# Hybrid mLSTM, attention and expert step on one core: tile 0's experts fetched beside the later mLSTM cells, mixers in two sets of buffers

## What is computed

```
h  = modulate(rmsnorm(x))
z  = h @ w_in                      # mLSTM q, k, v, o, gates; attention q, k, v
mix = [ mLSTM forward + backward, normed, times sigmoid(o)  ||  attention with sink ]
x1 = x + gate1 * (mix @ w_out)
h2 = modulate(rmsnorm(x1))
q  = h2 @ w_q                      # 8 heads x 2 halves x 128
eidx, gates = top-16 of 16 x 16 sums of the top-16 of both halves' scores
a  = gelu(h2 . u[eidx]) ;  y = x1 + gate2 * sum(gates * a * v[eidx])
```

## Time and profile before

| | |
|---|---|
| runs | 3685.03, 3685.37, 3698.58 us; median 3685.37 |
| span of the profiled execution | 3682.8 us, first to last instruction (no separate time of this execution is recorded) |
| granted TensorE clock, mean | 0.865 of 2.4 GHz |
| moved by DMA | 1365.12 MB, mean 371 GB/s over the span |
| first expert fetch | 664.09 us |
| chain that ended last | DMA 40%, TensorE (PE) 20%, VectorE (DVE) 15%, issue 4%, POOL 4%, ScalarE (ACT) 4% |

### The profile page before, as it was taken

How to read it: one execution, slowest core, us unless ns; L and a number is a source line. 1 busy time by engine, 2 the same in 40 slices (tenths; PEclk the granted TensorE clock), 3 DMA queues, 4 the chain that set the end, 5 groups by cost and what they waited for, 6 DMA issues and landing times.

```text
span 3682.8 us, 31091 instructions
## 1 busy us (share of the span) xinstructions
PE 2644.4 (72%) x9770; PEld 1042.0 (28%) x9770; DVE 2453.7 (67%) x5523; ACT 990.0 (27%) x2700; POOL 1459.0 (40%) x1300
## 2 busy tenths in 40 slices
PE   7999888687877878866566567557656755775655
PEld 3455567333333333312121112112111211221111
DVE  3666435776787678648857677685767768576655
ACT  1223333442433244422122122212212221221111
POOL 0110023443454455434444444444444444444443
PEclk9999889899989989889799789879977987987677
DMA  7222446899999999999999999999999999999999
GB/s 299 95 97 94 163 125 204 333 410 422 416 421 426 425 412 420 389 424 414 427 427 427 427 423 427 422 417 424 416 427 420 427 420 423 424 417 427 411 427 380
DMA packets 224537, 1365.12 MB, mean 371 GB/s; under 512 B 25194, under 2 KB 36074, under 8 KB 75890
## 3 DMA queue, kind: packets, MB, share of 16 engines
q0 software_dynamic: 165888, 1208.03, 78.4%
q1 hardware_dynamic: 50992, 134.74, 10.1%
q10 hardware_dynamic: 7492, 20.36, 1.4%
HBM read 1334.05 MB, written 28.99 MB: 370 GB/s over the span
## 4 chain that ended last, share of the span: by engine, by line
DMA 40%; PE 20%; DVE 15%; issue 4%; POOL 4%; ACT 4%; SPq 0%; ACTq 0%; POOLq 0%; DVEq 0%
DMA fx_ring<-arg_uv,fx_eidx 38%; PE fx_acc L1396 11%; DVE fx_ring L1846 8%; POOL fx_ring L1109 4%; PE at_sP L1241 3%; ACT fx_weighted_pick L1542 2%; PE at_aP L1203 1%; DMA rt_wq<-arg_w_q 1%; DVE rt_rest L1708 1%; DVE rt_ab L1710 1%; DVE rt_rest L1706 1%; DMA rt_w_q<-arg_w_q 1%; PE at_sP L1269 1%; ACT fx_gelu L1538 1%; PE at_sP L1187 1%
## 5 line engine op out<-in xcount | busy, mean ns | idle before, releaser
L1396 PE MATMUL fx_acc<-fx_ring,fx_weighted_pick 128*64 128x512 f32 x4608 | 1417.7, 747 | 929.8 <-ACT fx_weighted_pick L1542 908.3
L1109 POOL DMA_INDIRECT fx_ring<-arg_uv,fx_eidx x1152 | 1317.0, 1143 | 1634.7 <-PE fx_acc L1396 1444.5
L1846 DVE CUSTOM_DVE_ANT_0 fx_ring<-fx_ring,fx_h 128x1024 f32<-128x1024 f32 x1152 | 1411.8, 1237 | 774.0 <-DMA fx_ring<-arg_uv,fx_eidx 769.5
L1396 PEld LDWEIGHTS fx_acc<-fx_ring,fx_weighted_pick 128*64 128x64 f32 x4608 | 327.0, 158 | 1903.7 <-ACT fx_weighted_pick L1542 1368.4
L1538 ACT ACTIVATE fx_gelu<-fx_dot 128x2 f32<-128x2 f32 x576 | 117.1, 203 | 2116.2 <-DVE fx_dot L1846 2115.7
L424 PE MATMUL in_z<-w_in,in_hT 128*128 128x512 f32 (+1 forms) x864 | 352.4, 566 | 7.3 <-PEq L97 7.3
L1542 ACT ACTIVATE fx_weighted_pick<-fx_weighted_pick,fx_gelu 128x64 f32<-128x64 f32 x1152 | 338.0, 340 | 55.1 <-ACT fx_gelu L1538 2.2
L424 PEld LDWEIGHTS in_z<-w_in,in_hT 128*128 128x128 f32 x864 | 163.6, 192 | 177.3 <-issue 172.0
L1269 PE MATMUL rt_qP<-rt_w_q,rt_h2T 128*128 128x512 f32 x384 | 193.6, 629 | 9.4 <-DMA rt_w_q<-arg_w_q 9.4
L384 POOL COPY in_turned<-in_heads 128x320 f32<-128x320 f32 x9 | 9.1, 1010 | 320.1 <-DVE in_heads L579 320.1
L1241 PE MATMUL at_sP<-at_w_out,at_mixT 128*128 128x512 f32 x288 | 133.3, 606 | 0.9 <-DVE at_mixT L1601 0.9
(11 more groups left out here) (300 smaller groups left out, 2450.4 us busy)
## 6 DMA issues: line engine op xcount, KB each, us to landing
rt_wq<-arg_w_q SPq DMA_DIRECT2D x44, 512.0 KB, 7.8
fx_ring<-arg_uv,fx_eidx POOLq DMA_INDIRECT x1152, 12.7
in_ada_w<-arg_w_ada SPq DMA_DIRECT2D x32, 512.0 KB, 4.0
ml_qkT<-qkT_scratch SPq DMA_DIRECT2D x18, 512.0 KB, 4.2
ada_w<-arg_w_ada SPq DMA_DIRECT2D x8, 1024.0 KB, 13.8
w_in<-arg_w_in SPq DMA_DIRECT2D x16, 512.0 KB, 16.4
rt_w_q<-arg_w_q SPq DMA_DIRECT2D x16, 512.0 KB, 32.7
kv_scratch<-in_kv ACTq DMA_DIRECT2D x9, 768.0 KB, 3.3
```

The lines of the kernel that those rows point to most:

```text
L1109: pool.indirect_dma_start(out=ring[j][:], out_offset=None, in_=io.uv, in_offset=bass.IndirectOffsetOnAxis(ap=eidx[t % 2][:, i:i + 1], axis=0),
L1396: mm = pe.matmul(acc[b][cg * TOKS:(cg + 1) * TOKS, :], wsel[:, i % (2 * FILL), :], ring[i % GROUP][:, D + b * 512:D + (b + 1) * 512], star ...
L1846: dve.tensor_tensor_reduce(out=ring[j][:, 0:D], in0=ring[j][:, 0:D], in1=h2r[t % 2][cg][:], scale=1.0, scalar=0.0, op0=ALU.mult, op1=ALU.a ...
```

## The change

`drive` calls `begin` when the first half of tile 0's experts is chosen, without waiting for the cells. Ahead of it stand 29 cell steps now: route 0 has 16 in place of 43. Three more cell steps stand between `begin` and pair 0, and one stands behind each of the pairs 0 to 24. The mixer steps start behind pair 25, one per pair to the end of tile 0, and then one every other pair (tile 3: each pair below 30). Route 1 waits for mixer 1: no route steps behind pairs 17 to 39 of tile 0, then 1 and 2 in turn. So that ring and cells can be live together, cells get space of their own, in which later the mixers' second set of buffers and then w_q stand (`mixer_room`); mixer 0 has a set of its own, and w_out is loaded and scaled once for each set. Mixer 0 and route 0 use the experts' PSUM banks, the cells those of the later mixers. w_q is streamed for four tiles and loaded whole in pair 30 of tile 3.

```diff
-    STREAMED = 3
+    STREAMED = 4
+    ROOM = 17640
+    CELL_PAIRS = 25
...
     def due(t, r):
+        if t == 0:
+            return r >= CELL_PAIRS
         if t == STREAMED - 1:
             return r < WQ_AT
-        return t == 0 and r < SUBS or 17 <= r < 23 or r >= 51 or r % 2
+        return r % 2
 
     def pace(t, r):
+        if t == 0:
+            return int(r < 17) if r < CELL_PAIRS + SUBS else 1 + r % 2
         if t == STREAMED - 1:
             return int(r < 17 or r >= WQ_AT - 1) + int(r >= 48 and r % 2)
         return 1
...
     def cells_beside(k):
         if k < TURN:
             return 1
-        if k < TURN + 11:
-            return int(k % 3 > 0)
-        return 1 + int(k % 4 > 0)
+        return int(k % 3 == 0)
...
-        for _ in cells:
-            pass
         begin()
+        for _ in range(3):
+            next(cells)
...
                     next(steps)
                     left -= 1
+                if t == 0 and r < CELL_PAIRS:
+                    next(cells, None)
+                if t == 0 and r == CELL_PAIRS - 1:
+                    for _ in cells:
+                        pass
                 if due(t, r):
                     next(subs, None)
...
+        later = mixer_buffers(1)
+        with ExitStack() as room:
+            w_q = room.enter_context(nc.sbuf_tensor("rt_w_q", [P, KD, 2 * D], F32))
+        held = sb("mixer_room", [P, ROOM])
+        first = mixer_buffers(0)
...
-        eP = acc[0][:].rearrange("p (h n) -> p h n", n=P)
-        oE = acc[0][:].rearrange("p (h n) -> p h n", n=256)
-        R = [x[:].rearrange("p (h n) -> p h n", n=256) for x in (acc[1], qP[0], qP[1])]
+        eP = other[0][:].rearrange("p (h n) -> p h n", n=P)
+        oE = other[0][:].rearrange("p (h n) -> p h n", n=256)
+        R = [x[:].rearrange("p (h n) -> p h n", n=256) for x in (other[1], qP[0], qP[1])]
...
-        qP0, cP0 = ST, aP[:].rearrange("p (h n) -> p h n", n=P)
+        first.ST, later.ST = acc, other
+        qP0, cP0 = acc, aP[:].rearrange("p (h n) -> p h n", n=P)
...
+                def load_weights(cnd):
+                    m = later if cnd else first
+                    sp.dma_start(m.gate1[:], g.gate_dram[cnd:cnd + 1, :].to_broadcast([P, D])).then_inc(s_g1, 16)
+                    for k in range(KD):
+                        sp.dma_start(m.w_out[:, k, :], io.w_out[k * P:(k + 1) * P, :]).then_inc(s_wo, 16)
...
                         if k == (3 if t == 0 else 0):
                             load_h(t)
+                        if k == 0 and t == 1:
+                            load_head(1)
+                            load_weights(1)
...
                 def begin():
-                    pool.wait_ge(s_hd, UNITS)
-                    for d in range(2):
-                        pool.wait_ge(s_hst[d], 16 * TILES)
+                    pool.wait_ge(s_x1o, 16)
                     for n in range(DEPTH):
                         fetch(n)
...
-                        if 5 <= k < 5 + KD // 2 and t == 0:
+                        if 5 <= k < 5 + KD // 2 and t < 2:
```

More of the change, by code:

```diff
@@ L770, in mix_and_experts, with mixer_buffers, esb @@
         g.state.close()
+        def mixer_buffers(n):
+            with ExitStack() as room:
+                def esb(name, shape, dt=F32):
+                    return room.enter_context(nc.sbuf_tensor(f"{name}_{n}", shape, dt))
+                m = Names()
+                m.w_out = esb("at_w_out", [P, KD, D])
+                m.aq = esb("at_qT", [P, AH // 2, P])
+                m.mask = esb("at_mask", [P, 4 * P])
+                m.gate1 = esb("at_gate1", [P, D])
+                m.s = [esb(f"at_s{i}", [P, 4 * P]) for i in range(2)]
+                m.pT = [esb(f"at_pT{i}", [P, 4 * P]) for i in range(2)]
+                m.nmx = esb("at_negmax", [P, AH])
+                m.rs = esb("at_sum", [P, AH])
+                m.es = esb("at_sink_exp", [P, AH])
+                m.hq = esb("at_h_square", [P, MW])
+                m.sg = esb("at_sigmoid", [P, MW])
+                m.hr = esb("at_hrms", [P, MH])
+                m.mix = esb("at_mix", [P, D])
+                m.hs = m.mix[:, 0:MW]
+                m.mixT = esb("at_mixT", [P, KD, P])
+                m.x1 = esb("at_x1", [P, D])
+                m.xn = esb("at_xn", [P, D])
+            return m
+        later = mixer_buffers(1)
+        with ExitStack() as room:
+            w_q = room.enter_context(nc.sbuf_tensor("rt_w_q", [P, KD, 2 * D], F32))
+        held = sb("mixer_room", [P, ROOM])
+        first = mixer_buffers(0)
         ring = [sb(f"fx_ring{i}", [P, 2 * D]) for i in range(GROUP)]
@@ L774, in mix_and_experts @@
         gate2 = sb("fx_gate2", [P, D])
+        wq2 = [sb(f"rt_wq{i}", [P, HALF]) for i in range(WQ)]
+        ckT = sb("at_cache_kT", [P, P])
+        cv = sb("at_cache_v", [P, AKV * ADH])
+        sink = sb("at_sink", [P, AH])
+        nsink = sb("at_sink_negated", [P, AH])
+        small = sb("at_mh_g_rt_ss", [P, 2 * (KD // 2)])
+        mhg, ss = small[:, 0:KD // 2], small[:, KD // 2:KD // 2 + 1]
         h2r = [[sb(f"fx_h2_0_{i}", [P, D]) for i in range(NC)], h2r1]
@@ L941, in load_head @@
                 def load_head(t):
+                    m = first if t == 0 else later
                     if t:
                         sp.wait_ge(s_sc, t * AH)
-                    sp.dma_start(aq[:].rearrange("p h n -> p (h n)"), g.aqT_dram[t]).then_inc(s_q, 16)
+                    sp.dma_start(m.aq[:].rearrange("p h n -> p (h n)"), g.aqT_dram[t]).then_inc(s_q, 16)
                     if t in (0, 1, 2, TILES - 1):
@@ L947, in load_head @@
                             sp.wait_ge(s_nm, t * AH)
-                        sp.dma_start(mask[:], io.att_mask[t]).then_inc(s_mk, 16)
+                        sp.dma_start(m.mask[:], io.att_mask[t]).then_inc(s_mk, 16)
                 def load_h(t):
+                    m = first if t == 0 else later
                     if t < 2:
@@ L1068, in _ @@
                 load_head(0)
-                sp.dma_start(x1[:], io.x[0]).then_inc(s_x, 16)
-                sp.dma_start(gate1[:], g.gate_dram[0:0 + 1, :].to_broadcast([P, D])).then_inc(s_g1, 16)
-                for k in range(KD):
-                    sp.dma_start(w_out[:, k, :], io.w_out[k * P:(k + 1) * P, :]).then_inc(s_wo, 16)
+                sp.dma_start(first.x1[:], io.x[0]).then_inc(s_x, 16)
+                load_weights(0)
                 for m in range(2 * WQ):
@@ L1434, in route @@
                     for k in range(steps_of(t)):
-                        x1t = x1r if t else x1[:]
+                        x1t = x1r if t else first.x1[:]
                         if k == TURN - 3:
@@ L1811, in begin @@
                 def begin():
-                    for d in range(2):
-                        dve.wait_ge(s_hst[d], 16 * TILES)
+                    pass
                 def close(t):
```

163 lines of the change are left out of this document (69 added, 94 removed).

## The result

| | us | before beside it | ratio | 95% interval |
|---|---|---|---|---|
| changed kernel, median | 3766.08 (3760.27 to 3775.57) | 3689.97 (3685.03 to 3698.58) | 1.0213 | 1.0189 to 1.0237 |
| profiled execution, span | 3767.2 | 3682.8 | | |

A forecast was written before the change was run, and what follows sets the result against it. The prediction took DMA transfers to bound the kernel, so first-fetch time and bytes behind it set the end. Terms -49 + 56 + 6 + 12 + 6 - 2 gave +29 us, 3714 us, 0.8% slower; range 3681 to 3748.

The forecast's parts named there:

- Start (-49): Ahead of the experts: first fetch at 615 us in place of 664.09, 49 us earlier; ends 64 to 38 us.
- Bytes (+56): Behind the first fetch: 23.6 MB more to move at 421 GB/s, 56 us; ends 53 and 60.
- half pace: Tiles 1 and 2: a mixer step every other pair relieves the transfers, -2 us; ends -8 and 0.
- VectorE in pairs 0 to 16 (+6): Tile 0's first 17 pairs: VectorE needs 6.5 us a pair against 6.0 for bytes, +6 us; ends 0 and 17.
- So the cells' VectorE time alone fits: Pairs 0 to 16: VectorE's 5.5 us a pair, with a cell step, stays under the bytes' 6.0 us.
- the rival of an engine-bound tile 0: Tile 0: delays add up if POOL holds VectorE's next cell step; 3745 us at half the extra, 3760 at most; 16%.
- TensorE in pairs 40 to 63 (+12): End of tile 0: packed route and mixers give TensorE 157 us against 148 for bytes, +12 us; ends 0 and 28.
- POOL at pair 60 (+6): End of tile 0: tile 1's fetch waits two pairs for its first half of routing, +6 us; ends 0 and 8.
- Two PSUM sets and joined SBUF tiles cost nothing: the same operations: Whole kernel: the new buffer layout adds no time, as the operations stay the same.
- tiles 4 to 8 as before: Late tiles: a sign that would show the forecast, their times unchanged from the kernel before.

The follow-up runs named there:

- second trace: The changed kernel run again with no edit: 3769.16 us against 3690.74 for the kernel before, ratio 1.0220.
- w_q's part measured alone: Kernel before with w_q streamed for four tiles and mixers at half pace in tiles 1 to 3: 3705.12 us, ratio 1.0037.
- the buffers' 60 us: Changed kernel with the old order of work up to pair 63 of tile 0, its buffers and w_q streaming kept: 3750.60 us, 60 us over before.
- the run without mixer 2: Changed kernel with the ring on 512 bytes and mixer 2 moved from tile 0's pairs 40 to 63 to tile 1: 3710.24 us, ratio 1.0059.

## Why the prediction was wrong

**Start (-49): right, in part by luck.** Measured -47, and -53 in the second trace. The chain ran from 567.60 to about 617 us, 49 us, where 571 to 615 was forecast, 44 us. VectorE's busy time in it came out as planned, 37 us against the planned 36 (29 + 7, where the rows give 28 + 7). Its idle time did not: 12 us against 5.5 for the cells' waits and 2 for w_q. That the chain began 3 us sooner than planned made up for most of it.

**Bytes (+56): right.** 23.6 MB were forecast, and the traces have 23.0 MB and 54 us. w_q's part measured alone was 14 net of 20 gross, so half pace gave some 6 back (forecast -2, its end -8). w_out's second load was never run alone; what is left of the buffers' 60 us after 31 to 38 for the ring and 14 for w_q is 8 to 15, with an uncertainty as large as itself, and its bytes are worth 11.

**VectorE in pairs 0 to 16 (+6): right within its ends.** By the DMA records pairs 0 to 16 lost 4 us (1 before) and pairs 17 to 24, beside which the last cells are, 5 (2 before): 6 or 7 us more together. VectorE's group of dots in the first 100 us of the fetches:

```profile
L1876 DVE CUSTOM_DVE_ANT_0 fx_ring<-fx_ring,fx_h 128x1024 f32<-128x1024 f32 x30 | 41.4, 1414 | 4.4 <-DMA fx_ring<-arg_uv,fx_eidx 4.3
```

1414 ns a dot against 1237 in the earlier trace rows, 5 us more for 30 dots. POOL's product with k starts beside some of them, and such a dot takes longer:

```profile
663.64 1.05 POOL L1173 TENSOR_TENSOR ml_k<-ml_k,ml_cols 128x512 f32<-128x512 f32 x1
663.80 1.97 DVE L1876 CUSTOM_DVE_ANT_0 fx_ring<-fx_ring,fx_h 128x1024 f32<-128x1024 f32 x1
```

That the cells beside the pairs are cheap is shown by the difference of two runs: the changed kernel is 19 us faster than the same with all cells ahead of the fetches. Of the start's 47 us, the cells' bytes (10 MB) take 23 and the rest of the work about 5. The sentence "So the cells' VectorE time alone fits" was right, and the rival of an engine-bound tile 0 was wrong about the cells: that its 3745 came nearest to the measured time is luck. (Half of the extra by its own terms is 3737 and not 3745.)

**TensorE in pairs 40 to 63 (+12), and POOL at pair 60 (+6): the place was right, the size was not.** 18 us were forecast and 37 or 38 measured, in the traces and in the difference of two runs. The step that failed is "TensorE becomes the bound by 9 us if it never waits; at 0.9 busy it would be 174, 26 us over, less what the ring covers: four pairs of 4.95 us, less the 12.7 us from issue to landing, 7 us." It priced the stretch by TensorE's sum and took the waits as a tenth; its own numbers leave 26 - 7 = 19 us, and the term was then set at 12 without saying why. The fetches of pairs 44 and 63, which wait for the ends of pairs 40 and 59, start at 884.5 and 1030.9 us in the changed kernel: 7.7 us a pair, where 157 us were 6.5 a pair and even 174 only 7.25. From 884 to 1031 us TensorE is busy 127 of 147 us: 6.7 us a pair, near the sum of 6.5, and 1.05 idle. TensorE's busy time there also holds pieces at 1.2 GHz, as in the timeline above. Each pair had a mixer step and 1.4 route steps, each a round of engines in order, ahead of the next pair's products. The chain of waits from 920 to 1060 us in the changed kernel:

```profile
by line: DMA rt_wq<-arg_w_q 17.3%; PE rt_qP L1297 12.8%; issue 12.0%; PE fx_acc L1425 11.9%; PE at_sP L1269 10.1%; DVE fx_ring L1876 7.3%; POOL fx_ring L1139 3.5%; PE at_sP L1216 2.8%; PE rt_qP L1331 2.6%; PE at_aP L1232 2.5%; DVE rt_rest L
```

The same before, in 880 to 1040 us:

```profile
by line: DMA rt_wq<-arg_w_q 16.2%; DMA fx_ring<-arg_uv,fx_eidx 16.1%; DVE fx_ring L1846 13.3%; PE fx_acc L1396 12.9%; PE at_sP L1241 9.1%; PE rt_qP L1269 5.9%; issue 3.7%; PE at_aP L1203 3.5%; PE at_sP L1187 2.4%; POOL fx_ring L1109 1.7%; A
```

The fetches of experts, 16.1% before, are not among the first lines now, and w_q's pieces have much the same share in both. POOL's hold was priced in "POOL is held for two pairs, with three pairs in flight: about one pair's 5 us". It was 18.1 us. The two terms were added as if each stood alone, but the second grows with the first: where the pairs were faster, in the run without mixer 2, the hold was 10.6 us with the same packed route.

**"Two PSUM sets and joined SBUF tiles cost nothing: the same operations": wrong,** and the largest miss: 31 to 38 us for a term of 0 (ratios 1.0200 and 1.0220 against 1.0117 with the ring moved). The new room ahead of the ring is 70560 bytes long. It moved the ring from 28672 to 99232, which is 160 modulo 256, and every fetched row of 8 KB took some 5 ns more: 147456 rows on 16 engines, 4.9 ns by their means of 312.1 and 317.0, are 45 us of DMA time, 31 to 38 of them at the end. These rows hold the 16 engines for 78% of the span, so that rows longer by 1.6% are 1.2% of the kernel. No row of before could show it, but the addresses could be read from the code, and a term for a moved ring should have had ends other than 0 and 0. The prediction's own sign "tiles 4 to 8 as before" failed with it: they are 2 to 6 us longer each.

So the sum by its own terms: start -47, bytes 54 less 6 for half pace, VectorE and all else up to 920 us +9, packed stretch +37, ring +31 to 38, together +78 to 85 by runs and traces of different chips, where the spans differ by 84 and the medians by 76 to 78.

What stays open: why the cost off the boundary doesn't grow from 32 to 128 bytes (one more transaction fits, but was only argued), and w_out's share, which is a remainder. How the 37 us of the packed stretch divide between TensorE's load, its granted clock and the waits of the rounds was not separated.

## What to carry to other kernels

- In a kernel that is bound by transfers, start the buffers that the transfers write at multiples of 256 bytes (shown here for rows of 8 KB); a reshuffle of tensors ahead of them is a change of the inner loop.
- Price a stretch where one stream interleaves several chains by its rounds as well (steps a pair times what a round takes there), not by the busy time of the fullest engine alone. Moving the packing elsewhere moves its cost along, as two of these runs show.
- An early start that carries its own bytes with it gives them back: here some 47 us of start were 19 in hand, and the buffers that it needed cost 60.
